# Order of blocks and expert rows on TensorE, fourteen more rows on VectorE, and a re-spaced block table, in a two-block model kernel

## The chip, the cores and the metric

The kernel runs on one NeuronCore of one Trainium2 chip. The metric is device time in microseconds (us) of one execution; lower is better. The kernel before takes 2434.16 us, the median of 3 runs (2432.61 to 2436.7).

## The reference: what is computed

512 tokens of width 1024 pass a first block (gated delta net, sparse attention and a gated feed-forward with a short causal convolution) and a second one (a pooling and a convolution branch, an output projection and an expert layer), all in float32. The parts that matter here are the first block's feed-forward, the second block's branches, and the expert layer, whose reference is, cut to its core:

```python
def chunk_fn(hc):                                   # 128 tokens, 8 heads, 16 experts per head
    q = (hc @ w_query).reshape(PEER_CHUNK, PEER_HEADS, PEER_KEY_DIM)
    s1 = jnp.einsum('chk,nk->chn', q[..., :PEER_HALF_DIM], keys_1)
    s2 = jnp.einsum('chk,nk->chn', q[..., PEER_HALF_DIM:], keys_2)
    ...                                             # two top-16 lists, their 256 sums, top 16 of these
    gate = jax.nn.softmax(top_s.astype(jnp.float32), axis=-1).astype(hc.dtype)
    u = jnp.take(expert_u, experts, axis=0)
    act = jax.nn.gelu(jnp.einsum('chkd,cd->chk', u, hc))
    v = jnp.take(expert_v, experts, axis=0)
    return jnp.einsum('chk,chkd->cd', gate * act, v)
```

Every token fetches 128 experts of its own, so 128 tokens by 2048 floats (u and v side by side, 1 MB) come in for each of 4 x 8 x 16 = 512 steps. Such a step is called a row below.

## The kernel before, in words

The 512 tokens are two halves of 256 (the weights are used once for each) and four chunks of 128. All causal work of the first half goes ahead, so the expert layer of chunks 0 and 1 can start while the second half still has to pass the first block's feed-forward and all of the second block. The program is written out by hand for each engine; there is no scheduler. A common clock ties the engines: the pair `p` of rows 2p and 2p+1, from 0 to 255, 64 pairs a chunk. For each pair

- GpSimd issues the indirect DMA of each row into one of `RING` = 9 buffers of 1 MB; row g waits until row g-9 has been used (L2772, in order);
- VectorE multiplies the u half with the token and sums (`row_dot`, L2600), one step of the search for the experts of the head after next (`route`), and then the second half's work of this pair (its `beside(p)`);
- ScalarE makes the two weights (gelu, times the gate, L1747 and L1751) and for a row that TensorE weighs a 128 x 128 diagonal matrix of them (L1755) (`weigh_pair`), and then its own `beside(p)`;
- TensorE adds the v half to two PSUM banks with the diagonal as the stationary operand (`row_pair`, two matmuls of 512 columns a row), and then does the second half's blocks of this pair (its `beside(p)`).

A row that is in the list `SIDE` is not weighed by TensorE but by VectorE, with one multiply-add of 128 x 1024 into a buffer `side` (`side_row`, L1873), in VectorE's `beside` two pairs later; one matmul pair with the identity adds `side` to PSUM at a chunk's end. `SIDE` is built of `ONE` (pairs whose second row is on VectorE) and `BOTH` (pairs whose first row is too). Before, it has 81 rows.

A block is 128 output columns of a weight matrix: 8 matmuls (6 for the last third of `down`) of 256 or 258 columns with weights of 512 KB from a ring of three slots, loaded by SyncE in the order of `weight_order()`. The tables say at which pair TensorE does which block: `UP_AT` and `DOWN_AT` (the feed-forward's 41 remaining up and 24 down blocks), `QUERY_AT`, `WIN_AT` (28 blocks of the second block's input projection), `BRANCH_AT`, `WOUT_AT`. What has to follow a block is placed some pairs behind it: ScalarE takes an up block out of PSUM at `at + 2`, VectorE finishes it at `at + 3` (`expanded`), a down block is added by VectorE at `at + 2` (`add_part`). TensorE may start block t only when the slot and the bank of block t-3 are free, that is when ScalarE or VectorE has taken block t-3 out (`weights`). A layer norm of the convolution branch stands at pairs 78 to 86: `ln_mean` (78) and `ln_var` (82) on TensorE, `ln_root` (84) on ScalarE, `ln_scale` (85) and `ln_silu` (86) on VectorE; it is followed by the branch blocks, whose pooling half for three blocks (`branch_pool`) is at pair 86.

Of the kernel before, what the change touches and what calls it, by code (L numbers as in the profile page):

```python
# [21 lines left out]
KT = D // P  # L22
# [59 lines left out]
EARLY = 8  # L82
EARLY_UP = 3
# [5 lines left out]

def ffn_at(i):  # L90

    return 1 + 7 * (i + min(KT, (i + 3) // 6)) // 12


UP_AT = [-1 if b < EARLY_UP else ffn_at(b if b < 24 else b + KT) for b in range(2 * FT)]
DOWN_AT = [ffn_at(24 + q if q < KT else 44 + q) for q in range(CHUNKS * KT)]
MID_AT = 47
# [4 lines left out]
BRANCH_AT = [87 + m // 2 for m in range(KT)]  # L102
WOUT_AT = [93 + m // 2 for m in range(KT)]
NORM_AT = 99
QUERY_AT = [{m: 1 + 7 * (7 * (m - EARLY) + 3) // 12 for m in range(EARLY, 16)},
            {m: (103, 104, 108, 110)[m] if m < 4 else 112 + 4 * (m - 4) for m in range(16)}]


ONE = [*range(1, 48), *range(52, 61), *range(83, 97)]
BOTH = [*range(4, 46, 4)]  # L110
SIDE = sorted([2 * p + 1 for p in ONE] + [2 * p for p in BOTH])


def sides(g):

    return sum(q < g for q in SIDE)
# [7 lines left out]
def tensor_rows(p):  # L124

    return [k for k in range(BATCH) if BATCH * p + k not in SIDE]


def weighed(p):

    return sum(bool(tensor_rows(q)) for q in range(p))
# [10 lines left out]
def weight_order():  # L142
# [5 lines left out]
    for p in range(NC * TILE):  # L148
        order += [("query", 0, m) for m, q in QUERY_AT[0].items() if q == p]
        order += [("up", 1, b) for b, q in enumerate(UP_AT) if q == p]  # L150
# [3 lines left out]
        order += [("w_out_2", 1, m) for m, q in enumerate(WOUT_AT) if q == p]  # L154
        order += [("query", 1, m) for m, q in QUERY_AT[1].items() if q == p]
    return order
# [36 lines left out]
def build(nc, a, out):  # L193
    ctx = ExitStack()
    with ctx:
# [402 lines left out]
        def _(pe):  # L598
            def mm(o, l, r, start=True, stop=True):
                return nc.tensor.matmul(o, l, r, start=start, stop=stop)  # L600
# [124 lines left out]
            for m in range(24):  # L725
                j = m % SLOTS
# [13 lines left out]
                if 11 <= m < 19:  # L740
                    i = m - 11
# [366 lines left out]
            def square_sum(s, k):  # L1108

                pe.wait_ge(sq3_ready, KT * s + k + 1)  # L1110
                if k == 0:
                    pe.wait_ge(ln_std, s // 2 + 1)
                    if s == 1:
                        pe.wait_ge(std3_ready, 1)
                mm(PS[:, 5, :HF], ones, sq4[:, k % 4, :], k == 0, k == KT - 1).then_inc(sq3_used, 1)
# [10 lines left out]
            def key_scores(s, m):  # L1126

                pe.wait_ge(q_ready, 16 * s + m + 1)
                if 16 * s + m:
                    pe.wait_ge(sc2_ready, 16 * s + m)  # L1130
                for c in range(2):
                    ins = mm(PS[:, 6, c * P:(c + 1) * P], qT[:, m % 2, c * P:(c + 1) * P],
                             mat("keys1") if m % 2 == 0 else mat("keys2"))
                ins.then_inc(sc2_done, 1)
# [8 lines left out]
            def row_pair(p, start, stop):  # L1143

                rows = tensor_rows(p)
                if rows and p < LAST:
                    pe.wait_ge(diag_ready, weighed(p + 1))
                if start:
                    pe.wait_ge(hr_ready, 4)
                    if p:  # L1150
                        pe.wait_ge(prow_ready, 2 * (p // TILE))
                for k in rows:
                    r = (p * BATCH + k) % RING
                    if p == LAST:
                        pe.wait_ge(diag_ready, weighed(p) + k + 1)
                    for v in range(2):
                        ins = mm(PS[:, v, :], diag[:, p % NB, k, :],
                                 ring_e[:, r, D + v * S:D + (v + 1) * S],
                                 start and k == 0, stop and k == BATCH - 1)
                        if v or (p == LAST and k):  # L1160
                            ins.then_inc(rows_used, 1)

            def side_sum(c):

                pe.wait_ge(side_used, sides(BATCH * TILE * (c + 1)))
                for v in range(2):
                    mm(PS[:, v, :], ident, side[:, v * S:(v + 1) * S], False, False)
# [64 lines left out]
            def beside(p):  # L1232
# [4 lines left out]
                for s in range(2):  # L1237
                    for m, at in QUERY_AT[s].items():
                        if p == at + 3:
                            key_scores(s, m)  # L1240
                for m, at in QUERY_AT[0].items():
                    if p == at:
# [27 lines left out]
                for m, at in enumerate(WOUT_AT):  # L1270
                    if p == at:
                        project_out(1, m)
                    if p == at + 3:
                        square_sum(2, m)
                for m, at in QUERY_AT[1].items():
                    if p == at:
# [13 lines left out]
            for p in range(NC * TILE):  # L1290
                if p in (TILE - 1, 2 * TILE - 1):
                    side_sum(p // TILE)
                row_pair(p, p % TILE == 0, p % TILE == TILE - 1)
                beside(p)


        @block.scalar
        def _(act):
# [485 lines left out]
            def beside(p):  # L1784
# [6 lines left out]
                for s in range(2):  # L1791
                    for m, at in QUERY_AT[s].items():
                        if p == at + 2:
# [1106 lines left out]
```

## Time and profile before

| what | before |
|---|---|
| median of 3 runs | 2434.16 us |
| the profiled execution, its own time | 2429.77 us |
| its span in the profile | 2428.1 us |
| TensorE busy (matmuls) | 2197.1 us, 90% |
| VectorE busy | 1663.0 us, 68% |
| ScalarE, GpSimd busy | 748.1 us, 632.2 us |
| HBM read | 750.59 MB |

The span is the time from the first to the last instruction that the profiler recorded; 1.7 us of the execution lie around it. Row work begins at 920.9 us (first indirect DMA issued) and fills the rest. TensorE is recorded with two MATMUL records for each float32 matmul of the program, so that a block is x16 and a row is x4 in the trace. Busy shares over the whole span mix stages with different limits; the views below are taken by stage. The time at which a matmul group starts after the one before it is its cost; the durations printed for a group also hold the pipeline's tail.

### The profile page before, as it was taken

Reading aid. Unit: us, or ns where it says so; the run is one execution under the profiler, and the core shown is the slowest. Engines: PE = TensorE matmul, PEld = TensorE weight load, DVE = VectorE, ACT = ScalarE, POOL = GpSimd, SP = SyncE. Lnnn points to the kernel's source line nnn. Section 1 sums busy time; section 2 is a strip of 40 time slices with the busy share of each in tenths; the row PEclk is TensorE's granted clock in tenths of the full one; section 3 lists DMA queues with packets and bytes.
Section 4 is the critical chain, followed back from the end, with each engine's and each line's share of the span. In section 5 each row is a group of like instructions: output and inputs, shape, how many; then the busy total and the mean of one; then the engine's idle time right before and its main releaser. Section 6 shows DMA issues by size and latency. Waiting matters only on the chain.

```text
span 2428.1 us, 25277 instructions
## 1 busy us (share of the span) xinstructions
PE 2197.1 (90%) x8236; PEld 1449.2 (60%) x8236; DVE 1663.0 (68%) x3734; ACT 748.1 (31%) x2109; POOL 632.2 (26%) x606
## 2 busy tenths in 40 slices
PE   7999998999999998999998999899888977778776
PEld 3444787788888886777774556565444432333332
DVE  5563645476657737988878998877666666676654
ACT  2321335421102212322324223244333333342322
POOL 1100000000110002323335343344434443444442
PEclk9999999999999999999999999999999999999999
DMA  8631020366774348999999999999999999999997
GB/s 344 200 120 56 32 70 1 111 230 223 266 271 148 132 156 349 414 401 380 398 400 420 413 395 379 370 404 420 421 420 421 422 421 421 419 417 420 421 415 306
DMA packets 131784, 754.22 MB, mean 311 GB/s; under 512 B 14544, under 2 KB 14672, under 8 KB 65616
## 3 DMA queue, kind: packets, MB, share of 16 engines
q0 software_dynamic: 87456, 588.90, 60.0%
q1 hardware_dynamic: 44208, 163.84, 18.6%
q8 instruction: 61, 1.00, 0.2%
q14 instruction: 59, 0.48, 0.1%
HBM read 750.59 MB, written 2.10 MB: 310 GB/s over the span
## 4 chain that ended last, share of the span: by engine, by line
PE 52%; DMA 27%; DVE 14%; ACT 4%; issue 2%; POOL 0%; DVEq 0%; SPq 0%; ACTq 0%; POOLq 0%
PE PS L600 51%; DMA arena<-experts_dram,ecur 23%; DVE arena L2600 4%; DVE arena L1873 3%; DVE h_all L1873 2%; DMA ring<-up_dram 1%; ACT const L1755 1%; DVE arena L1867 1%; ACT arena L1751 1%; ACT L1747 1%; DMA ring<-down_dram 1%; DMA ring<-branch_dram 1%; DVE h_all L1867 1%; DMA ring<-w_out_dram 1%; DMA xT<-x_dram 0%
## 5 line engine op out<-in xcount | busy, mean ns | idle before, releaser
L600 PE MATMUL PS<-arena,const 128*128 128x512 f32 (+2 forms) x1764 | 832.8, 618 | 170.4 <-ACT const L1755 161.5
L600 PE MATMUL PS<-h_all,ring 128*128 128x256 f32 (+2 forms) x3584 | 881.7, 403 | 13.9 <-DVE ring L1873 4.2
L2772 POOL DMA_INDIRECT arena<-experts_dram,ecur x512 | 583.0, 1139 | 1111.1 <-PE PS L600 702.4
L2600 DVE CUSTOM_DVE_ANT_0 arena<-arena 128x1024 f32<-128x1024 f32 x512 | 625.7, 1222 | 289.3 <-DMA arena<-experts_dram,ecur 286.0
L600 PEld LDWEIGHTS PS<-h_all,ring 128*128 128x128 f32 x3584 | 678.2, 190 | 224.9 <-issue 132.6
L600 PEld LDWEIGHTS PS<-arena,const 128*128 128x128 f32 x1764 | 335.4, 196 | 595.8 <-issue 345.7
L1747 ACT ACTIVATE arena<-arena 128x2 f32<-128x2 f32 x255 | 51.6, 202 | 727.6 <-DVE arena L2600 727.1
L600 PE MATMUL PS<-arena,ring 128*128 128x256 f32 x1088 | 243.7, 383 | 6.0 <-DMA ring<-down_dram 3.2
L600 PEld LDWEIGHTS PS<-arena,ring 128*128 128x128 f32 x1088 | 207.3, 192 | 39.6 <-DMA ring<-down_dram 5.1
L1755 ACT ACTIVATE const<-const,arena 128x128 f32<-128x128 f32 x429 | 148.4, 387 | 0.0
L600 PE MATMUL PS<-arena 128*128 128x128 f32 (+4 forms) x936 | 137.8, 299 | 8.5 <-DVE arena L1867 3.4
L600 PEld LDWEIGHTS PS<-arena 128*128 128x128 f32 (+2 forms) x936 | 118.0, 194 | 28.8 <-issue 12.8
L1924 DVE CUSTOM_DVE_ANT_0 arena<-arena 128x1024 f32<-128x1024 f32 x92 | 109.0, 1222 | 26.0 <-DMA arena<-ada_dram 24.7
L1751 ACT ACTIVATE arena<-arena 128x1 f32<-128x1 f32 x510 | 122.3, 287 | 8.4
L1873 DVE SCALAR_TENSOR_TENSOR arena<-arena 128x1024 f32<-128x1024 f32 (+3 forms) x118 | 107.8, 914 | 1.4
L1873 DVE SCALAR_TENSOR_TENSOR arena<-PS,param,arena 128x255 f32<-128x255 f32 (+3 forms) x128 | 72.3, 565 | 42.7 <-ACT arena L1376 31.7
L1873 DVE SCALAR_TENSOR_TENSOR xT<-PS,mod,xT 128x256 f32<-128x256 f32 x71 | 34.2, 482 | 96.4 <-PE PS L600 95.6
L2752 POOL DMA_DIRECT2D arena<-crow_dram x1 | 0.5, 528 | 316.1 <-ACT arena L1540 316.1
L2759 POOL DMA_DIRECT2D arena<-ada_dram x44 | 23.3, 529 | 222.2 <-DVE mod L1924 209.3
L1867 DVE TENSOR_TENSOR arena<-arena 128x512 f32<-128x512 f32 (+7 forms) x165 | 70.7, 429 | 5.2 <-ACT arena L1398 2.7
L1747 ACT ACT_TABLE_LOAD x37 | 47.5, 1283 | 65.1 <-DVE arena L2600 47.7
L1873 DVE SCALAR_TENSOR_TENSOR arena<-ring,param,arena 128x256 f32<-128x256 f32 x120 | 58.2, 485 | 4.3
(273 smaller groups left out, 1481.0 us busy)
## 6 DMA issues: line engine op xcount, KB each, us to landing
ring<-up_dram SPq DMA_DIRECT2D x88, 512.0 KB, 3.3
ring<-w_in_dram SPq DMA_DIRECT2D x80, 512.0 KB, 3.8
arena<-ada_dram POOLq DMA_DIRECT2D x80, 512.0 KB, 5.1
ring<-w_out_dram SPq DMA_DIRECT2D x32, 512.0 KB, 5.0
ring<-query_dram SPq DMA_DIRECT2D x32, 512.0 KB
ring<-down_dram SPq DMA_DIRECT2D x16, 704.0 KB, 5.8
ring<-branch_dram SPq DMA_DIRECT2D x16, 512.0 KB
arena<-experts_dram,ecur POOLq DMA_INDIRECT x512
```

The costliest lines, as they stand in the source:

```text
L600: return nc.tensor.matmul(o, l, r, start=start, stop=stop)
L1747: A(wts[:, b, :], dots[:, b, :], ACT.Gelu_apprx_tanh).then_inc(gelu_ready, 1)
L1751: A(wts[:, b, k:k + 1], wts[:, b, k:k + 1], ACT.Copy, scale=gcur[:, r % 3, j:j + 1]).then_inc(w_ready2, 1)
L1755: A(diag[:, b, k, :], ident, ACT.Copy, scale=wts[:, b, k:k + 1]).then_inc(diag_ready if k == rows[-1] else act_step, 1)
L1867: return V.tensor_tensor(out=o, in0=x, in1=y, op=op)
L1873: return V.scalar_tensor_tensor(out=o, in0=x, scalar=s_, in1=y, op0=op0, op1=op1)
L1924: V.tensor_tensor_reduce(out=w, in0=w, in1=row, scale=1.0, scalar=0.0, op0=MUL, op1=ADD, accum_out=mod[:, blk, t:t + 1]).then_inc(used, 1)
L2600: V.tensor_tensor_reduce(out=u, in0=u, in1=hrow[:, (r // HEADS) % 2, :], scale=1.0, scalar=0.0, op0=MUL, op1=ADD, accum_out=dots[:, p % NB ...
L2752: pool.dma_start(crow_2, a["crow"][1][:, 0:D]).then_inc(late_loaded, 16)
L2759: pool.dma_start(ring_2[:, j, :], a["ada_2"][bass.ds(i * SLOTS + j, 1)].rearrange("o p n -> p (o n)")).then_inc(slot_2_ready[j], 16)
L2772: nc.gpsimd.indirect_dma_start(out=ring_e[:, g % RING, :], out_offset=None, in_=a["experts"], in_offset=bass.IndirectOffsetOnAxis(ap=ecur[ ...
```

## The change

Three things change together. On TensorE, `beside(p)` is called before `row_pair(p)`, so the blocks of a pair stand ahead of the matmuls that weigh its rows. `SIDE` gets 14 more rows, nine in pairs 14 to 39 and five in pairs 81 to 99: 95 rows instead of 81. And the blocks of the feed-forward are spread at 5 blocks in 3 pairs from pair 1 on, where they stood at 12 blocks in 7 pairs from pair 3 on; the eight query blocks among them move by a pair at most.

```diff
 def ffn_at(i):
 
-    return 1 + 7 * (i + min(KT, (i + 3) // 6)) // 12
+    j = i - EARLY_UP
+    return 1 + 3 * (j + min(KT, (j + 3) // 6)) // 5
...
-QUERY_AT = [{m: 1 + 7 * (7 * (m - EARLY) + 3) // 12 for m in range(EARLY, 16)},
+QUERY_AT = [{m: 1 + 3 * (7 * (m - EARLY) + 3) // 5 for m in range(EARLY, 16)},
             {m: (103, 104, 108, 110)[m] if m < 4 else 112 + 4 * (m - 4) for m in range(16)}]
...
-ONE = [*range(1, 48), *range(52, 61), *range(83, 97)]
-BOTH = [*range(4, 46, 4)]
+ONE = [*range(1, 48), *range(52, 61), *range(81, 100)]
+BOTH = [*range(4, 46, 4), 14, 18, 19, 22, 23, 30, 34, 38, 39]
...
                 if p in (TILE - 1, 2 * TILE - 1):
                     side_sum(p // TILE)
+                beside(p)
                 row_pair(p, p % TILE == 0, p % TILE == TILE - 1)
-                beside(p)
```

The first place is TensorE at pairs 0 to 5, before. In these rows (instruction, what it writes and reads, columns, how many) `arena,const 128x512` is the weighing of rows, x2 for each, `h_all,ring 128x258` an up block (x8), `h_all,ring 128x256` a query block, and `mats,arena` the key scores:

```order
L600 MATMUL PS<-arena,const 128x512 x4
L600 MATMUL PS<-mats,arena 128x128 x2
L600 MATMUL PS<-arena,const 128x512 x4
L600 MATMUL PS<-h_all,ring 128x256 x8
L600 MATMUL PS<-arena,const 128x512 x2
L600 MATMUL PS<-h_all,ring 128x258 x24
L600 MATMUL PS<-arena,const 128x512 x2
```

And TensorE at pairs 0 to 5 in the changed kernel:

```order
L601 MATMUL PS<-mats,arena 128x128 x2
L601 MATMUL PS<-arena,const 128x512 x4
L601 MATMUL PS<-h_all,ring 128x258 x16
L601 MATMUL PS<-arena,const 128x512 x2
L601 MATMUL PS<-h_all,ring 128x256 x8
L601 MATMUL PS<-h_all,ring 128x258 x8
L601 MATMUL PS<-arena,const 128x512 x2
L601 MATMUL PS<-h_all,ring 128x258 x8
L601 MATMUL PS<-arena,const 128x512 x2
L601 MATMUL PS<-h_all,ring 128x258 x16
```

Two up blocks now stand between the rows of pair 0 and the row of pair 1, where before the rows of pairs 0, 1 and 2 stood together. Up to and with pair 4, six up blocks are done instead of three.

The second place is TensorE at pairs 81 to 87 before, where `sq,const 128x256` is `ln_var` and `h_all,ring 128x256` is an input projection block (x8) or the pooling half of three branch blocks (x12):

```order
L600 MATMUL PS<-arena,const 128x512 x4
L600 MATMUL PS<-h_all,ring 128x256 x8
L600 MATMUL PS<-arena,const 128x512 x4
L600 MATMUL PS<-h_all,ring 128x256 x8
L600 MATMUL PS<-sq,const 128x256 x4
L600 MATMUL PS<-arena,const 128x512 x8
L600 MATMUL PS<-h_all,ring 128x256 x12
L600 MATMUL PS<-arena,const 128x512 x2
```

And TensorE at pairs 81 to 87 in the changed kernel:

```order
L601 MATMUL PS<-h_all,ring 128x256 x8
L601 MATMUL PS<-arena,const 128x512 x2
L601 MATMUL PS<-h_all,ring 128x256 x8
L601 MATMUL PS<-sq,const 128x256 x4
L601 MATMUL PS<-arena,const 128x512 x8
L601 MATMUL PS<-h_all,ring 128x256 x12
L601 MATMUL PS<-arena,const 128x512 x2
```

Four matmuls, the rows of pair 82, went from before `ln_var` to behind it (one of them to VectorE), pair 81 keeps one row on TensorE, and the pooling halves now stand ahead of pair 86's row.

## Rows read from the trace of the kernel before

**Rows 1.** The page, busy time, share of the span and instructions of each engine.
```profile
PE 2197.1 (90%) x8236; PEld 1449.2 (60%) x8236; DVE 1663.0 (68%) x3734; ACT 748.1 (31%) x2109; POOL 632.2 (26%) x606
```

**Rows 2.** Windows of the row work: length, busy time by engine, TensorE's clock, DMA share, GB/s.
```profile
941.00:1300.00 359.00, 336.81 (x1364) 255.88 (x1364) 310.48 (x667) 110.12 (x321) 128.26 (x101) 0.99 1.00 401
1300.00:1500.00 200.00, 189.03 (x642) 122.45 (x643) 187.23 (x445) 63.13 (x205) 76.03 (x62) 0.98 1.00 400
1500.00:1550.00 50.00, 41.04 (x136) 27.06 (x135) 38.84 (x90) 16.22 (x46) 19.30 (x16) 0.90 0.95 367
1550.00:1700.00 150.00, 147.61 (x533) 95.88 (x532) 110.61 (x260) 56.72 (x166) 62.04 (x51) 1.00 1.00 408
1700.00:2350.00 650.00, 527.03 (x1272) 238.64 (x1272) 437.05 (x1088) 225.01 (x740) 266.48 (x253) 0.96 1.01 421
2350.00:2428.00 78.00, 55.61 (x122) 21.73 (x120) 37.97 (x64) 21.50 (x78) 22.42 (x23) 0.97 0.79 327
```

**Rows 3.** Windows, pairs 6 to 45, columns as in Rows 2.
```profile
960.00:1260.00 300.00, 290.86 (x1227) 229.30 (x1225) 258.08 (x543) 84.78 (x250) 102.11 (x82) 1.00 0.99 399
```

**Rows 4.** Timeline, TensorE, pairs 13 and 14: start, us, instruction, count.
```profile
1036.88 7.14 PE L600 MATMUL PS<-h_all,ring 128*128 128x258 f32 x32
1043.86 1.88 PE L600 MATMUL PS<-arena,const 128*128 128x512 f32 x4
1045.57 3.65 PE L600 MATMUL PS<-h_all,ring 128*128 128x258 f32 x16
```

**Rows 5.** Timeline, VectorE, pairs 14 to 18, columns as in Rows 4.
```profile
1025.59 1.23 DVE L2600 CUSTOM_DVE_ANT_0 arena<-arena 128x1024 f32<-128x1024 f32 x1
...
1045.88 2.04 DVE L1873 SCALAR_TENSOR_TENSOR ring<-PS,param,ring 128x256 f32<-128x256 f32 x4
...
1051.51 1.26 DVE L1873 SCALAR_TENSOR_TENSOR arena<-arena 128x1024 f32<-128x1024 f32 x1
...
1056.33 1.21 DVE L2600 CUSTOM_DVE_ANT_0 arena<-arena 128x1024 f32<-128x1024 f32 x1
```

**Rows 6.** Timeline, GpSimd, issue of row 37; in brackets idle time and releaser.
```profile
1046.01 0.94 POOL L2772 DMA_INDIRECT arena<-experts_dram,ecur  x1 [6.57 <-PE PS L600]
```

**Rows 7.** Waits, 950 to 1300 us: who for whom, us, times, longest.
```profile
POOL arena L2772 <- PE PS L600: 136.8, 31, 17.9
...
POOL arena L2772 <- DVE arena L1873: 88.9, 29, 8.0
...
DVE xT L1873 <- PE PS L600: 25.8, 10, 4.1
```

**Rows 8.** Timeline, VectorE, the second down block of pair 17.
```profile
1075.93 0.48 DVE L1873 SCALAR_TENSOR_TENSOR xT<-PS,mod,xT 128x256 f32<-128x256 f32 x1 [2.97 <-PE PS L600]
```

**Rows 9.** Timeline, TensorE, first rows of pair 0 and on.
```profile
946.10 5.08 PE L600 MATMUL PS<-arena,const 128*128 128x512 f32 x8 [7.17 <-ACT const L1755]
```

**Rows 10.** Timeline, GpSimd, issue of rows 11 and 13.
```profile
953.62 0.94 POOL L2772 DMA_INDIRECT arena<-experts_dram,ecur  x1 [1.01 <-PE PS L600]
...
956.26 0.95 POOL L2772 DMA_INDIRECT arena<-experts_dram,ecur  x1 [0.30 <-issue]
```

**Rows 11.** Timeline, TensorE, pairs 82 to 86.
```profile
1506.32 3.60 PE L600 MATMUL PS<-arena,const 128*128 128x512 f32 x8
1509.75 3.62 PE L600 MATMUL PS<-h_all,ring 128*128 128x256 f32 x16
1513.20 1.89 PE L600 MATMUL PS<-sq,const 128*128 128x256 f32 x8
...
1525.52 3.78 PE L600 MATMUL PS<-arena,const 128*128 128x512 f32 x4 [5.28 <-ACT const L1755]
```

**Rows 12.** Timeline, VectorE, pair 85's side row and the layer norm's scale.
```profile
1510.78 0.75 DVE L1870 TENSOR_SCALAR arena<-arena 128x1024 f32<-128x1024 f32 x1
1515.69 1.75 DVE L2406 RECIPROCAL rs<-rs 128x256 f32<-128x256 f32 x1 [4.17 <-ACT rs L1612]
```

## The prediction, made before the changed kernel had run

> **What bounds the kernel now.** I began with the page: TensorE is busy for 90% of the span and VectorE for 68% [rows 1]. That says little, since the change touches only pairs 0 to 99, so I went to windows of the row work and read the last column first. From 1700 to 2350 us nothing but rows is left and the DMA engines move 421 GB/s at a share of 1.01: full. That rate is my yardstick. A stretch of length T at a rate r holds T x (1 - r/421) of DMA time in which nothing was moved, and since the bytes are fixed this is the most that the stretch can give back [rows 2]:
>
> - 941 to 1300 us, the feed-forward of the second half: 359 x (1 - 401/421) = 17.1 us;
> - 1300 to 1500 us, input projection and convolution taps: 200 x (1 - 400/421) = 10.0 us;
> - 1500 to 1550 us, the layer norm: 50 x (1 - 367/421) = 6.4 us;
> - 1550 to 1700 us, branches and output projection: 150 x (1 - 408/421) = 4.6 us;
> - 1700 to 2350 us: none. What is won before 1700 us stays won, since full DMA work behind it only starts earlier.
>
> Who holds the DMA up? In pairs 6 to 45 (300 us) TensorE is busy for 290.9 us, VectorE for 258.1 us [rows 3]. TensorE's groups follow each other without a gap: two blocks from 1036.88 to 1043.86, so 3.49 us a block; one row from 1043.86 to 1045.57, so 1.71 us a row [rows 4]. GpSimd, which refills the ring, waited 136.8 us in 31 waits for TensorE to free a row buffer and 88.9 us in 29 for VectorE [rows 7]. So TensorE is the nearest bound here by a narrow margin: it is 97% busy, DMA runs at 95% of its yardstick.
>
> How far TensorE is behind shows in one pair. VectorE forms pair 14's first product at 1025.59; TensorE weighs that row at 1043.86, 18.3 us later, and ends at 1045.57; GpSimd then issues row 37 (nine rows on) at 1046.01, and VectorE reaches its product at 1056.33, 10.3 us after the issue [rows 4 to 6]. Meanwhile VectorE, at the end of pair 16, finishes the two up blocks of pair 13 at 1045.88, right after TensorE ended them at 1043.86 [rows 4, 5]. Its place is three pairs behind theirs, so TensorE's lag is as large as the tables allow. For a down block the place is only two pairs behind, and there VectorE must stop: 25.8 us in ten waits, one of them up to 1075.93 [rows 7, 8].
>
> From 1300 to 1500 us both TensorE (189.0 of 200 us) and VectorE (187.2) are nearly full [rows 2]; the change takes nothing from either there until pair 81.
>
> From 1500 us on it is the layer norm. TensorE weighs pair 82's two rows at 1506.32, does a block at 1509.75 and `ln_var` from 1513.20; ScalarE's root follows, and VectorE, which was done with its side row at 1510.78 + 0.75 = 1511.5, waits 4.17 us to 1515.69 [rows 11, 12]. TensorE then runs dry itself, 5.28 us before 1525.52, because pair 86's diagonal comes late [rows 11].
>
> **The change, part by part.**
>
> *Nine rows to VectorE in pairs 14 to 39.* TensorE: 9 x 1.71 = 15.4 us less. VectorE: 9 x 1.26 = 11.3 us more, by the side row at 1051.51 [rows 5]. VectorE has 300 - 258.1 = 41.9 us free in that stretch [rows 3], so the cover is there on the whole, but not at every pair. If the cover were gone the whole 11.3 us would lie on the path. Five of the nine are in pairs 14 to 23, around the first down blocks, and three in 34 to 39 around the next ones, where VectorE stood waiting for TensorE [rows 7, 8]. I take 2 us as given back, between 0 and 11.3.
>
> *Blocks before rows.* No work is added. Of what TensorE issues, only the order changes; the SyncE queue's weight loads keep their rule (free after block t-3) and change places only as the tables do. Two effects. (1) VectorE's and ScalarE's waits for a block end one row, 1.71 us, sooner against TensorE's rows. (2) A row buffer is freed behind its own pair's blocks, up to 2 x 3.49 = 7.0 us later. What queues behind that is GpSimd's in-order issue, and behind it the DMA engines. With TensorE at its allowed lag, row 2p+9 would be issued 7 us later against the product of pair p+4, and 10.3 us from issue to product [rows 5, 6] leaves no room. So VectorE's lead over TensorE must shrink from about three pairs to a little over two. That costs TensorE nothing as long as it still finds block t-3 taken out; I take 2 us for jitter in this narrower play, between 0 and 7 (one full lag of one pair).
>
> *Earlier start, even spacing.* Before, TensorE waits 7.17 us up to 946.10 for the first diagonal, then weighs the rows of pairs 0 to 2 together, and rows 11 and 13 are issued at 953.62 and 956.26 [rows 9, 10]. Now pair 1's row stands behind two blocks: row 11 about 7.0 us later. The blocks are work that has to be done anyway and TensorE was short of nothing else, but the row queue runs dry for part of it. The weights' loads fill some. I take 3 us, between 0 and 7.0.
>
> Sum for pairs 0 to 47: 15.4 - 2 - 2 - 3 = 8.4 us, under the cap of 17.1 us. From the bounds: 15.4 at best, 15.4 - 11.3 - 7 - 7 = -9.9 at worst.
>
> *Five rows to VectorE in pairs 81 to 99, and the new order at the layer norm.* `ln_var` comes after one row less of pair 81 (1.71 us) and before pair 82's rows, which took 1509.75 - 1506.32 = 3.43 us: 5.1 us sooner. VectorE's wait is 4.17 us and vanishes [rows 12]; its two more side rows there, 2 x 1.26 us, fall into pairs in which it waits for rows to land. So 4.2 us. The pooling halves of three branch blocks now fill TensorE's 5.28 us wait [rows 11], and pairs 97 to 99 lose 3 x 1.71 = 5.1 us on TensorE; at most 6.4 + 4.6 - 4.2 = 6.8 us more could come of it, but I see no wait that surely ends sooner, the branch blocks hanging on their weights. I take 0, between 0 and 6.8. If the cover fails on VectorE, 5 x 1.26 = 6.3 us come off.
>
> The sum is 8.4 + 4.2 = 12.6, say 12 us off the span of 2428.1 us: 2416 us, 2418 us for that execution. The median of the runs is 4.4 us above the profiled execution, so 2434.2 - 12 = 2422 us.
>
> **A page against the rows.** TensorE's 290.9 busy us of 300 are matmul time; its weight loads are 229.3 us, 76% [rows 3]. The Trainium skill (Trainium Kernel Development and Optimization, Performance Expectations) calls matmul busy time a poor measure of how near to its limit TensorE is, and the share of weight loads a good one. By that, TensorE had a quarter of its time free and the 15.4 us would buy nothing: the sum would be the 4.2 us of the layer norm alone. I side with the touching groups [rows 4], and keep it as a rival below. On DMA, the skill (DMA: Bandwidth & Descriptors, Specifications) gives one core about 358 GB/s from HBM; by it no stretch had anything to give back. The trace disagrees with 421 GB/s over 650 us [rows 2].
>
> **The rivals.**
>
> - *The gain stays in the ring.* The new order's later release costs both upper bounds (7 + 7 us) while the layer norm still pays: 15.4 - 14 - 2 + 4.2 = 3.6 us, 2431 us, no measurable change. For it: GpSimd already waits 136.8 us for TensorE. Against it: the lag shrinks instead of adding up. 15%.
> - *TensorE is not the limit* in pairs 6 to 45 and VectorE or DMA takes its place at once: 4.2 us, 2430 us. For it: three engines are within a few per cent of each other [rows 2, 3]. Against it: the long waits are for TensorE. 8%. (The skill's rule on weight loads, above, would come out here.)
> - *The ring becomes the loop, slower.* From a freed buffer: 0.4 us to the issue, 10.3 us to the product, some 4.5 us to the end of that pair on VectorE (1.2 for the product, 1.3 or 2.5 for side rows, 1 to 2 for the up blocks [rows 5]), two blocks 7.0 us, a row 1.7 us = 23.9 us, and that is a round of three pairs, where before, with rows ahead of blocks, it was one of four. 23.9 / 3 = 8.0 us a pair against 300 us / 40 = 7.5 us now. It decides when the issue takes more than about 9 us to become a product. Over the 28 pairs with up blocks: 28 x 0.5 = 14 us, less the layer norm's 4.2: 2444 us. Against it: with the DMA queue shorter a row lands sooner. 12%.
> - *Nearly all of the idle DMA time comes back*: 17.1 + 6.4 + 3 = 26 us, 2408 us. 5%.
>
> **Numbers.** The forecast, some 6 to 20 us off, has 60%; its own range is 2414 to 2428. Changes of 0.2%, 4.9 us, are about what a measurement of this kernel tells from none. Faster by more: 60 + 5 + 3 (parts of the first two) = 68%. Same: 12 + 8 = 20%. Slower: 12%. Leaving out the largest gain and most of the slow case gives 2412 to 2435.
>
> **What would show it.** Right: the rate from the first row to pair 47 rises from 401 to about 410 GB/s and pair 47 comes some 8 us sooner; TensorE's row records fall by 14 x 4; TensorE waits a little more and GpSimd's waits for it are more but shorter; VectorE's wait before its reciprocal of the layer norm is gone; the part behind 1700 us is the same at 421 GB/s, only shifted. Wrong: a first stretch at 401 GB/s or less, with VectorE waiting for rows to land (ring loop), or VectorE busy for over 96% (it took TensorE's place), or gaps of many us on TensorE that end with VectorE's take-out of an up block.

## The result, and the profile after: slower by 0.8%

The changed kernel takes **2452.1 us** (median of four runs, 2450.0 to 2453.4) where the kernel before takes 2433.4 us beside it (four runs, 2432.1 to 2436.7). The ratio is 1.0076, with a 95% interval of 1.0064 to 1.0089, or 15.6 to 21.7 us. The forecast was 2422 us with a range up to 2435; sign and size were both wrong. The profiled execution took 2453.36 us with a span of 2451.7 us.

The page's line of busy time, which answers to [rows 1]:

```profile
PE 2185.5 (89%) x8180; PEld 1444.9 (59%) x8180; DVE 1682.3 (69%) x3748; ACT 743.9 (30%) x2095; POOL 627.2 (26%) x606
```

TensorE lost 56 matmuls, the 14 x 4 of the fourteen rows, and 11.6 us of busy time. Yet the span grew by 23.6 us. The windows of the row work (columns as in [rows 2]) show where:

```profile
941.00:1300.00 359.00, 320.00 (x1296) 250.05 (x1296) 303.64 (x629) 93.28 (x280) 116.22 (x91) 0.96 0.96 375
1300.00:1500.00 200.00, 184.28 (x604) 116.18 (x604) 186.31 (x435) 66.68 (x205) 76.40 (x64) 0.97 1.00 404
1500.00:1550.00 50.00, 43.90 (x153) 28.63 (x152) 40.23 (x95) 19.48 (x55) 17.68 (x15) 0.99 0.95 368
1550.00:1700.00 150.00, 134.22 (x474) 90.55 (x474) 121.15 (x277) 49.96 (x150) 59.96 (x49) 0.93 0.99 397
1700.00:2350.00 650.00, 529.56 (x1326) 242.91 (x1325) 437.32 (x1100) 228.08 (x744) 268.69 (x255) 0.98 1.01 420
```

The first line answers for nearly all of it. From 941 to 1300 us DMA moved 375 GB/s where it had moved 401, so this stretch lacks 359 x (401 - 375) / 401 = 23.3 us of the old kernel's DMA work. The second moves a little more (404 against 400, 2.0 us), the third is as before, the fourth lacks 150 x (408 - 397) / 408 = 4.0 us, the fifth is as before. (From the second line on, the same window holds work that stands some 22 us later in the program.) TensorE, VectorE and DMA have all become *less* busy in the inner stretch that answers to [rows 3]:

```profile
960.00:1260.00 300.00, 272.96 (x1129) 217.46 (x1128) 251.14 (x513) 77.90 (x229) 94.66 (x76) 0.97 0.95 370
```

TensorE fell from 97% to 91%, VectorE from 86% to 84%, DMA from 399 to 370 GB/s. By the rate a pair now takes 7.5 x 399 / 370 = 8.1 us. All three are slower and none is full, which suggests that they wait for each other in a circle. The waits from 950 to 1300 us (who waits for whom, us in total, times, longest) answer to [rows 7]:

```profile
POOL arena L2773 <- PE PS L601: 192.6, 26, 18.2
...
POOL arena L2773 <- DVE arena L1874: 39.2, 15, 4.7
...
DVE arena L2601 <- DMA arena<-experts_dram,ecur: 29.5, 22, 5.0
...
PE PS L601 <- DVE ring L1874: 18.1, 8, 4.0
DVE xT L1874 <- PE PS L601: 15.3, 6, 6.0
```

Two of these waits were short in the kernel before:

```profile
DVE arena L2600 <- DMA arena<-experts_dram,ecur: 7.5, 7, 2.5
...
PE PS L600 <- DVE ring L1873: 4.2, 3, 1.6
```

VectorE waits 29.5 us for rows to land (7.5 before), TensorE 18.1 us for VectorE to take a block out (4.2 before). GpSimd waits 56 us more for TensorE to free a row and 50 us less for VectorE (88.9 before), so most of its idle time has only changed the engine that it is put down to. Follow one turn of the circle in the timelines (start, us, instruction, count, idle time and releaser). TensorE, pairs 11 to 15:

```profile
1038.94 1.88 PE L601 MATMUL PS<-arena,const 128*128 128x512 f32 x4
1040.66 10.63 PE L601 MATMUL PS<-h_all,ring 128*128 128x258 f32 x48
1051.12 1.88 PE L601 MATMUL PS<-arena,const 128*128 128x512 f32 x4
...
1061.47 8.79 PE L601 MATMUL PS<-h_all,ring 128*128 128x258 f32 x32 [4.00 <-DVE ring L1874]
1070.11 1.88 PE L601 MATMUL PS<-arena,const 128*128 128x512 f32 x4
```

GpSimd, the issues of rows 31 to 33 and of row 39 (row r goes into the buffer of row r - 9):

```profile
1041.10 1.05 POOL L2773 DMA_INDIRECT arena<-experts_dram,ecur  x1 [8.24 <-PE PS L601]
1042.45 1.09 POOL L2773 DMA_INDIRECT arena<-experts_dram,ecur  x1 [0.30 <-issue]
1043.84 0.94 POOL L2773 DMA_INDIRECT arena<-experts_dram,ecur  x1 [0.30 <-issue]
...
1072.26 0.94 POOL L2773 DMA_INDIRECT arena<-experts_dram,ecur  x1 [10.71 <-PE PS L601]
```

VectorE, the products of rows 31 to 33 and the take-out that ends pair 16:

```profile
1047.04 1.23 DVE L2601 CUSTOM_DVE_ANT_0 arena<-arena 128x1024 f32<-128x1024 f32 x1 [0.61 <-DMA arena<-experts_dram,ecur]
...
1051.52 1.23 DVE L2601 CUSTOM_DVE_ANT_0 arena<-arena 128x1024 f32<-128x1024 f32 x1 [0.85 <-DMA arena<-experts_dram,ecur]
...
1055.16 1.22 DVE L2601 CUSTOM_DVE_ANT_0 arena<-arena 128x1024 f32<-128x1024 f32 x1 [2.00 <-DMA arena<-experts_dram,ecur]
...
1060.32 2.04 DVE L1874 SCALAR_TENSOR_TENSOR ring<-PS,param,ring 128x256 f32<-128x256 f32 x4
```

TensorE weighs pair 11's row at 1038.94 and frees it at 1040.66. Row 31 goes out 0.4 us later, with rows 32 and 33 behind it; row 32's buffer had been free since VectorE's side row at 1032.12 + 1.28 = 1033.4, but GpSimd issues in order. VectorE waits for each of them to land (0.61, 0.85, 2.00 us), so pair 16's second product is at 1055.16 and, behind two side rows (one of them among the nine new ones), its take-out only at 1060.32. TensorE has stood 4.00 us for that take-out, does its blocks from 1061.47, and only behind them, at 1070.11, comes the row of pair 15. It is free at 1071.8, and row 39 goes out at 1072.26. From one freed row to the other are 31.2 us for four pairs: 7.8 us a pair, with nobody full. In the kernel before, the row stood ahead of the blocks, and TensorE's three waits for take-outs were 1.6 us at most.

TensorE's granted clock has a part in this. TensorE stands idle up to 1061.47, and then (columns as in [rows 2], the clock third from the end)

```profile
1061.40:1064.00 2.60, 2.52 (x6) 2.09 (x7) 2.50 (x7) 0.00 (x0) 0.15 (x1) 0.50 1.01 414
```

the clock is 0.50, that is 1.2 GHz instead of 2.4. The two blocks from 1061.47 to the row at 1070.11 cost 8.64 us where two blocks before cost 6.98 [rows 4]. Without these 1.66 us this turn would take 29.5 us, or 7.4 us a pair, about the pace of the kernel before: in this turn the circle's slack is used up, and the clock adds the loss. From 960 to 1260 us the clock fell so five times, each time when TensorE had just stood idle, for take-outs or for weights; in the kernel before it stayed at 1.00 there. As an estimate, the mean of 0.97 is worth at most 0.03 x 300 = 9 us of TensorE's time. So a part of the loss comes by way of the clock, as a consequence of the idle time; no run holds the two apart. A lower mean clock alone does not bring the loss: `f1_takeout`, below, has 0.96 from 941 to 1300 us as well (0.99 from 960 to 1260) and moves 398 GB/s against 375.

### The profile page after: what moved, and what is told of

Read it like the earlier page. It is cut to its first block, busy times and chain, and to the rows that moved or that the text cites. A ratio compares the mean times of both kernels' runs of the same rounds, so it can differ in the third digit from the quotient of the medians.

```text
span 2451.7 us, 25183 instructions
## 1 busy us (share of the span) xinstructions
PE 2185.5 (89%) x8180; PEld 1444.9 (59%) x8180; DVE 1682.3 (69%) x3748; ACT 743.9 (30%) x2095; POOL 627.2 (26%) x606
## 4 chain that ended last, share of the span: by engine, by line
PE 48%; DMA 28%; DVE 15%; ACT 4%; issue 3%; POOL 1%; DVEq 0%; SPq 0%; ACTq 0%; POOLq 0%
PE PS L601 48%; DMA arena<-experts_dram,ecur 25%; DVE arena L2601 4%; DVE arena L1874 4%; DVE h_all L1874 2%; DMA ring<-down_dram 2%; DVE arena L1868 1%; ACT const L1756 1%; ACT arena L1752 1%; DVE h_all L1868 1%; DMA ring<-up_dram 1%; POOL arena L2773 1%; ACT L1748 1%; DVE ring L1874 1%; DMA xT<-x_dram 0%
## 5 line engine op out<-in xcount | busy, mean ns | idle before, releaser
L601 PE MATMUL PS<-arena,const 128*128 128x512 f32 (+2 forms) x1708 | 804.9, 615 | 172.1 <-ACT const L1756 167.4
L601 PE MATMUL PS<-h_all,ring 128*128 128x256 f32 (+2 forms) x3584 | 891.9, 407 | 28.0 <-DVE ring L1874 23.9
L601 PEld LDWEIGHTS PS<-arena,const 128*128 128x128 f32 x1708 | 322.6, 196 | 586.6 <-issue 324.3
L601 PEld LDWEIGHTS PS<-arena,ring 128*128 128x128 f32 x1088 | 209.4, 194 | 47.1 <-DMA ring<-down_dram 12.7
L1874 DVE SCALAR_TENSOR_TENSOR arena<-arena 128x1024 f32<-128x1024 f32 (+3 forms) x132 | 125.7, 952 | 2.4
L2760 POOL DMA_DIRECT2D arena<-ada_dram x44 | 23.3, 529 | 222.1 <-DVE mod L1925 209.2
```

What stands on the lines that cost most here:

```text
L1874: return V.scalar_tensor_tensor(out=o, in0=x, scalar=s_, in1=y, op0=op0, op1=op1)
L2760: pool.dma_start(ring_2[:, j, :], a["ada_2"][bass.ds(i * SLOTS + j, 1)].rearrange("o p n -> p (o n)")).then_inc(slot_2_ready[j], 16)
```

## The experiments

"us" is (ratio - 1) x 2433.4. The last three columns come from the timelines: when VectorE starts its first product of the pair, counted from its first product of pair 0, minus the same in the kernel before. For pair 48 of the changed kernel these are the rows

```profile
940.47 1.23 DVE L2601 CUSTOM_DVE_ANT_0 arena<-arena 128x1024 f32<-128x1024 f32 x1
...
1301.08 1.22 DVE L2601 CUSTOM_DVE_ANT_0 arena<-arena 128x1024 f32<-128x1024 f32 x1
```

or 360.6 us, against 1279.07 - 940.61 = 338.5 us before: 22 us late.

| kernel | median, us | ratio (95%) | us | pair 8 | pair 48 | pair 255 |
|---|---|---|---|---|---|---|
| changed kernel | 2452.1 | 1.0076 (1.0064 to 1.0089) | +18.5 | +7.2 | +22.2 | +23.7 |
| e1_order | 2453.1 | 1.0088 (1.0067 to 1.0109) | +21.4 | +1.3 | +16.4 | +16.6 |
| e2_side | 2423.1 | 0.9952 (0.9936 to 0.9969) | -11.7 | -0.9 | -2.5 | -7.0 |
| e3_spacing | 2432.0 | 0.9986 (0.9976 to 0.9996) | -3.4 | +4.9 | +2.5 | +1.9 |
| e4_side_spacing | 2424.4 | 0.9960 (0.9946 to 0.9974) | -9.7 | +4.6 | -2.2 | -6.8 |
| f1_takeout | 2436.1 | 1.0011 (1.0000 to 1.0022) | +2.7 | +10.5 | +3.1 | +5.6 |
| f2_ring8_old | 2456.8 | 1.0086 (1.0069 to 1.0103) | +20.9 | +6.2 | +17.8 | +26.3 |
| f3_ring8_new | 2518.2 | 1.0331 (1.0305 to 1.0357) | +80.5 | +11.3 | +62.3 | +87.7 |
| f4_late | 2434.0 | 0.9999 (0.9987 to 1.0011) | -0.2 | +4.6 | +2.5 | +5.3 |
| f5_down | 2426.5 | 0.9970 (0.9961 to 0.9980) | -7.3 | +5.2 | 0.0 | -5.0 |
| f6_up | 2441.8 | 1.0046 (1.0030 to 1.0061) | +11.2 | +6.9 | +13.4 | +8.5 |
| f7_norm | 2423.2 | 0.9962 (0.9951 to 0.9973) | -9.2 | +4.6 | -2.4 | -10.2 |
| g1_side_early | 2420.7 | 0.9948 (0.9930 to 0.9969) | -12.7 | +3.6 | -2.5 | -8.8 |

The profile columns come from one execution each. Up to pair 47 `e4_side_spacing` and `f4_late` are the same program and differ by 4.7 us at pair 48: differences below about 5 us between two kernels in those columns say little. Inside one profile, from one pair to another, a step that returns in several kernels says more.

### The parts apart: e1_order, e2_side, e3_spacing, e4_side_spacing

`e1_order` is the kernel before with

```diff
+                beside(p)
                 row_pair(p, p % TILE == 0, p % TILE == TILE - 1)
-                beside(p)
```

> Only the new order on TensorE (blocks of a pair ahead of its rows), tables and side rows as before. Theory A (the ring loop: a row buffer is freed one pair's blocks later, so 9 buffers are too few) expects most or more of the whole loss: 15 to 35 us slower than before, since TensorE has no relief from side rows. Theory B (the fourteen side rows overload VectorE) expects no change within 5 us. Theory C (the earlier start of the blocks starves the row queue) expects at most 5 us slower.

`e2_side` is the kernel before with the fourteen rows alone:

```diff
-ONE = [*range(1, 48), *range(52, 61), *range(83, 97)]
-BOTH = [*range(4, 46, 4)]
+ONE = [*range(1, 48), *range(52, 61), *range(81, 100)]
+BOTH = [*range(4, 46, 4), 14, 18, 19, 22, 23, 30, 34, 38, 39]
```

> Only the fourteen more side rows, order and tables as before. Theory A expects 4 to 12 us faster than before, by TensorE's 15.4 us of relief in the first stretch. Theory B expects 10 to 20 us slower. Theory C expects no loss, 0 to 10 us faster.

`e3_spacing` is the kernel before with the spacing alone:

```diff
-    return 1 + 7 * (i + min(KT, (i + 3) // 6)) // 12
+    j = i - EARLY_UP
+    return 1 + 3 * (j + min(KT, (j + 3) // 6)) // 5
...
-QUERY_AT = [{m: 1 + 7 * (7 * (m - EARLY) + 3) // 12 for m in range(EARLY, 16)},
+QUERY_AT = [{m: 1 + 3 * (7 * (m - EARLY) + 3) // 5 for m in range(EARLY, 16)},
```

> Only the new spacing of the feed-forward's blocks (from pair 1, five in three pairs), order and side rows as before. Theory A expects within 5 us of before. Theory B expects the same. Theory C expects 8 us slower or more.

`e4_side_spacing` has both of these and the old order; it is the changed kernel with `beside(p)` put back behind `row_pair`.

> The changed kernel without its new order on TensorE: side rows and spacing. Theory A expects faster than before by 4 to 12 us, so some 25 us faster than the changed kernel. Theory B and theory C expect it slower than before, near the changed kernel's 2452 us.

Measured: the order alone costs 21 us, the side rows gain 12, the spacing gains 3. Side rows and spacing together gain 10, and the order put on top of them costs 28. The sum of the three parts would be +6.3; all together are +18.5, so the order is dearer with the other two than without. The windows from 960 to 1260 us, first of `e1_order`, then of `e2_side`:

```profile
960.00:1260.00 300.00, 282.98 (x1178) 222.96 (x1176) 247.58 (x518) 81.48 (x239) 91.95 (x77) 0.98 0.96 377
```
```profile
960.00:1260.00 300.00, 286.25 (x1212) 228.14 (x1211) 272.73 (x556) 82.45 (x244) 111.30 (x83) 0.99 1.00 402
```

The order alone does to this stretch most of what the whole change did: 377 GB/s and TensorE at 94%, with TensorE waiting 15.8 us for take-outs and VectorE 38.2 us for rows to land (950 to 1300 us). So the order is the culprit, and neither the side rows nor the start are: by pair 8 `e1_order` is 1.3 us late.

`e2_side` tells a second thing. TensorE has less to do and is at 95%, VectorE at 91%, and DMA moves 402 GB/s instead of 399, at a share of 1.00. By pair 48 only 2.5 us are won, of the nine rows' 15.4. The rest is won where the layer norm is; VectorE's reciprocal, which waited 4.17 us [rows 12], waits 0.71:

```profile
1513.24 1.75 DVE L2406 RECIPROCAL rs<-rs 128x256 f32<-128x256 f32 x1 [0.71 <-ACT rs L1612]
```

From pair 80 to 88 `e2_side` goes from 4.0 to 7.5 us ahead; `e4_side_spacing`, `f5_down` and `f7_norm` gain 3.5, 3.5 and 3.7 us in the same eight pairs.

### Does the circle run through the take-outs and the ring? f1_takeout, f2_ring8_old, f3_ring8_new

If the circle is the cause, shortening it at another place must give time back, and taking a buffer out of it must cost more in the new order than in the old one. `f1_takeout` is the changed kernel with the second half's feed-forward take-outs one pair sooner on VectorE and ScalarE:

```diff
-                    if p == at + 2 and m >= EARLY_UP:
+                    if p == at + 1 and m >= EARLY_UP:
...
-                    if p == max(UP_AT[2 * t], UP_AT[2 * t + 1]) + 4:
+                    if p == max(UP_AT[2 * t], UP_AT[2 * t + 1]) + 3:
...
-                    if p == at + 3 and m >= EARLY_UP:
+                    if p == at + 2 and m >= EARLY_UP:
```

The `tanh_gate`, `square_block(1, ...)` and `add_part` lines lose one pair in the same way.

> The changed kernel with ScalarE's and VectorE's work on the feed-forward's up and down blocks one pair earlier (taken out at the block's pair + 1, finished at + 2, down blocks added at + 1). If the loss is a round of ring and take-outs (free buffer, issue, landing, product, take-out, block, rows), this gives the round one pair more, and TensorE's idle time falls: 10 to 25 us faster than the changed kernel's 2452 us. If the late release by itself costs the time, whoever waits behind it, the take-outs' place changes nothing beyond 5 us. If VectorE then has to wait for TensorE at each block instead, it is slower than the changed kernel by 5 us or more.

`f2_ring8_old` is `e4_side_spacing`, `f3_ring8_new` the changed kernel, each with

```diff
-RING = 9
+RING = 8
```

> Side rows and spacing with the old order, and a ring of 8 row buffers instead of 9 (against 2424 us with 9). The ring theory expects a cost already here, 3 to 12 us, as half a pair of the play is gone. A theory in which the ring is deep enough in either order expects under 3 us.

> The changed kernel (new order) with a ring of 8 row buffers instead of 9 (against 2452 us with 9). The ring theory expects that the lost buffer costs clearly more than under the old order: 15 to 40 us more than the changed kernel. If the loss is TensorE standing at its blocks' waits and not the ring, it costs about what it costs under the old order.

Measured: `f1_takeout` gives 16 us of the 28 back. Its window and its waits, 950 to 1300 us:

```profile
960.00:1260.00 300.00, 287.41 (x1223) 228.88 (x1222) 269.44 (x551) 82.34 (x247) 112.73 (x83) 0.99 0.99 397
```
```profile
POOL arena L2773 <- DVE arena L1874: 116.0, 33, 7.3
...
POOL arena L2773 <- PE PS L601: 99.8, 21, 18.6
...
DVE arena L2601 <- DMA arena<-experts_dram,ecur: 7.3, 9, 1.7
...
PE PS L601 <- DVE ring L1874: 5.1, 2, 2.9
```

TensorE's wait for take-outs fell from 18.1 to 5.1 us, VectorE's for rows from 29.5 to 7.3, and GpSimd's for TensorE from 192.6 to 99.8. No work was removed and TensorE's order of blocks and rows is the same; only VectorE's and ScalarE's work on the blocks stands a pair earlier, and all three waits shrank together. This is what a circle through the take-outs predicts. The control, the same edit in the old order, was not run; in `e4_side_spacing` TensorE waited 3.2 us for take-outs in one wait, so there was little for it to shorten. By pair 48 `f1_takeout` is 3.1 us behind the kernel before instead of 22.2. Of the 12 us that it stays over `e4_side_spacing`, its profile has 5 us at pair 48, all of them there since the first eight pairs, and 7 us behind pair 48, where the edit does not reach.

One buffer fewer costs 30.6 us in the old order and 62 us in the new. The direction is the expected one, both sizes are missed: the theory had 3 to 12 and 15 to 40 us. So nine buffers were a tight ring in the old order too. The windows of `f2_ring8_old` and `f3_ring8_new`, and of `f3_ring8_new` the waits:

```profile
960.00:1260.00 300.00, 279.33 (x1170) 222.32 (x1169) 259.66 (x529) 78.96 (x230) 97.56 (x76) 0.98 0.98 383
```
```profile
960.00:1260.00 300.00, 253.42 (x1019) 200.36 (x1017) 227.81 (x464) 71.16 (x209) 81.83 (x68) 0.93 0.88 335
```
```profile
DVE arena L2601 <- DMA arena<-experts_dram,ecur: 62.6, 37, 4.6
...
PE PS L601 <- DVE ring L1874: 45.3, 12, 6.3
```

With eight buffers both waits of the circle more than double (29.5 to 62.6, 18.1 to 45.3 us), and DMA is down to 335 GB/s. The old order with eight buffers (383 GB/s) still beats, from 960 to 1260 us, the new order with nine (370): there the new order costs more than a buffer of the ring.

### In which pairs? f4_late, f5_down, f6_up, f7_norm

These are `e4_side_spacing` with the new order in some pairs only:

```diff
+                if COND:
+                    beside(p)
                 row_pair(p, p % TILE == 0, p % TILE == TILE - 1)
-                beside(p)
+                if not (COND):
+                    beside(p)
```

COND is `p >= 48` in `f4_late`, pairs 16 to 20 and 35 to 44 (down blocks) in `f5_down`, pairs 1 to 15 and 21 to 34 (up blocks) in `f6_up`, and pairs 82 and 86 (the layer norm's) in `f7_norm`.

> Side rows and spacing, with the new order on TensorE only from pair 48 on. The ring theory places the whole loss in pairs 0 to 47, so it expects the time of side rows and spacing alone, 2424 us, within 4 us. If the new order also pays at the layer norm, as the prediction had it, 2 to 5 us faster than 2424. If the order costs in the branches too (blocks two a pair there), 3 to 8 us slower.

> Side rows and spacing, with the new order on TensorE only in the pairs of down blocks (16 to 20, 35 to 44). A down block is taken out a pair earlier than an up block, so the round through ring and take-outs is a pair longer there. The ring theory expects a small share of the first stretch's 24 us: 0 to 8 us slower than side rows and spacing alone (2424 us). If the order costs the same wherever it stands, 8 to 10 us.

> Side rows and spacing, with the new order on TensorE only in the pairs of up blocks (1 to 15, 21 to 34). The ring theory expects most of the first stretch's 24 us here: 14 to 24 us slower than 2424 us. If the order costs the same wherever it stands, 15 us; if the down pairs are the dear ones (TensorE then is nearest to VectorE), under 10 us.

> Side rows and spacing, with the new order on TensorE only in pairs 82 and 86: ln_var ahead of pair 82's row, the pooling halves ahead of pair 86's. The prediction's step on the layer norm expects up to 4 us below side rows and spacing alone (2424 us), if the side rows have not already taken that wait. The ring theory, by which the late part of the new order costs through the rows of pairs 79 to 83 that are freed later, expects no loss here: within 3 us of 2424.

Measured against `e4_side_spacing` (-9.7 us): `f6_up` +20.9, `f4_late` +9.5, `f5_down` +2.4, `f7_norm` +0.5. The first three cover nearly all pairs, and their sum, 32.8, is near the 28 us of the new order everywhere. Windows of `f6_up`, then of `f5_down`:

```profile
960.00:1260.00 300.00, 276.58 (x1155) 219.72 (x1154) 257.98 (x527) 78.35 (x229) 96.03 (x78) 0.98 0.97 381
```
```profile
960.00:1260.00 300.00, 284.44 (x1210) 226.23 (x1209) 269.84 (x550) 82.50 (x245) 113.11 (x81) 0.99 1.00 400
```

So the up pairs carry it. `f5_down` cannot be told from `e4_side_spacing` (their intervals overlap), though it puts blocks ahead of rows in 15 pairs. `f7_norm` shows no gain and no cost from the order at the layer norm itself that could be told from none. `f4_late` missed its expectation: the theory had placed the whole loss in pairs 0 to 47 and allowed 4 us. The late part is only half settled: the ten runs of `f4_late` lie between 2426 and 2439 us, and in its profile 4.7 of 12.1 us against `e4_side_spacing` stand there before the programs differ. It goes from 2.5 us late at pair 48 to 5.3 at the end while `e4_side_spacing` goes from 2.2 to 6.8 ahead, so 7.4 us lie behind pair 48, not in pairs 82 and 86 themselves. Its profile has most of them at one place: `f4_late` is 2.7 us late at pair 83 and 8.9 at pair 84, while `e4_side_spacing` goes from 2.7 to 1.8 us ahead and `f7_norm` from 3.6 to 2.7; `f1_takeout` and the changed kernel make the same step of 6.4 us. Before it GpSimd in `f4_late` had waited for TensorE to free pair 78's row,

```profile
1490.01 1.05 POOL L2776 DMA_INDIRECT arena<-experts_dram,ecur  x1 [7.85 <-PE PS L601]
```

which points at the same late release in the input projection's pairs 78 to 80. No run tried the order in these pairs alone.

### Who limits once the old order is back? g1_side_early

`e4_side_spacing` with VectorE's side rows a pair sooner, so that it frees them sooner:

```diff
-                for g in range(BATCH * (p - 2), BATCH * (p - 1)):
+                for g in range(BATCH * (p - 1), BATCH * p):
```

> Side rows and spacing with the old order, and VectorE's side rows one pair earlier (pair p - 1 instead of p - 2), so that the buffers of these 95 rows are free a pair sooner. The ring theory expects a gain, 2 to 8 us below 2424 us, since GpSimd waited 112 us for VectorE's rows there; if VectorE instead has to wait for ScalarE's weights, 5 us slower or more.

GpSimd's waits, 950 to 1300 us, of `e4_side_spacing` and then of `g1_side_early`:

```profile
POOL arena L2773 <- DVE arena L1874: 112.1, 31, 10.6
...
POOL arena L2773 <- PE PS L601: 106.8, 24, 18.3
```
```profile
POOL arena L2773 <- PE PS L601: 181.7, 33, 18.5
...
POOL arena L2773 <- DVE arena L1874: 30.6, 12, 5.8
```

81.5 us of waiting for VectorE went away and 74.9 us of waiting for TensorE came in their place: the same idle time under another name. The time is 2420.7 us, the lowest here, 0.5% below the kernel before (interval 0.3 to 0.7%); against `e4_side_spacing` the intervals overlap, and the gain is not told from none. In this kernel DMA moved 405 GB/s from 941 to 1300 us, the most of all fourteen kernels.

## Why the prediction was wrong, step by step

**The step that failed: "blocks before rows".** It said: "That costs TensorE nothing as long as it still finds block t-3 taken out; I take 2 us". TensorE did not find it taken out. The order cost 21 us alone and 28 us with the rest, where I allowed 0 to 7. The error was to treat the later release as a shift that is paid once, "one full lag of one pair". A release that is late in every pair is paid in every pair as soon as the way from it back to itself has no slack. All parts of that way stood in the prediction: the in-order issue, the landing, the product, the take-out, the block that waits for it. The rival on the ring followed them round; the sum followed them up to the product and stopped. What the runs showed instead is TensorE waiting 18.1 us for take-outs where it had waited 4.2, and a loss in every turn.

**The rival "the ring becomes the loop" was what happened.** It gave 8.0 us a pair; the rate says 8.1. It priced the loop at 14 us over 28 pairs with up blocks; from pair 8 to 48 the changed kernel lost 22.2 - 7.2 = 15 us. That both come out so near is in part luck, since the turn is another one than it drew. It had a round of three pairs and 23.9 us. The turn in the timelines spans four pairs: 0.4 us to the issue, 14.1 to row 33's product (row 33 waits in the queue behind rows 31 and 32), 6.3 to the block that gets its bank back, 8.6 for two blocks, 1.7 for the row, 31.2 us in all with the 1.66 us of slow clock, on which the rival had nothing. It even named the pairs, which `f6_up` and `f5_down` bear out. It had 12%, because "with the DMA queue shorter a row lands sooner". That came true in part: row 31 needed 5.9 us from issue to product, rows 32 and 33, queued behind it, 9.1 and 11.3. It did not open the circle, since the take-out of the whole pair waits for the last of them. What the rival lacked beside this were the start (7.2 us at pair 8) and a price behind pair 48; it took off 4.2 us there.

**Nine side rows: mis-sized.** I took 15.4 - 2 = 13.4 us. By pair 48 `e2_side` is 2.5 us ahead, in one profile. Here the yardstick was wrong. I read 401 GB/s against 421 as idle DMA time of 17.1 us, though the share of DMA in that same row was 1.00. In none of fourteen kernels did that stretch pass 405 GB/s. The mean hides two kinds of time. The rate of the kernel before in 40 slices of 9 us, 941 to 1300 us:

```profile
GB/s 418 374 417 422 419 418 415 420 419 395 391 419 423 412 378 367 409 258 428 414 410 394 405 362 424 414 362 411 416 383 369 422 421 401 316 425 416 417 424 424
```

25 of the 40 slices stand at 410 or more, with weights coming in beside the rows, and eight below 380. That weights are in the traffic does not by itself set the lower mean. The kernel before moved 400 GB/s from 1300 to 1500 us, with 13.1 of 79.9 MB on the weights' queue (16%); `f7_norm` moved 419 from 1550 to 1700 us, with 9.3 of 62.8 MB (15%):

```profile
1550.00:1700.00 150.00, 141.95 (x502) 90.38 (x501) 112.61 (x259) 57.27 (x167) 64.38 (x54) 0.98 1.01 419
```

What makes the low slices stays open. So the second rival, that something else takes TensorE's place at once, describes the side rows in the feed-forward. The Trainium skill (Trainium Kernel Development and Optimization, Performance Expectations), by which matmul busy time is a poor measure of TensorE's nearness to its limit, would have come out nearer than my reading of the touching groups did. What it gives as the better measure, the share of weight loads, this case does not test: it stood at 76% before and what stood beside it once TensorE had less to do was a DMA share of 1.00.

**Layer norm: 4.2 us, right in size, wrong in cause.** `e2_side` gains 3.5 us from pair 80 to 88, and the 4.17 us wait shrinks to 0.71 with the old order. That pair 81 and its neighbours have a row less on TensorE is the likely reason; the new order added nothing (`f7_norm`). In the changed kernel the wait is gone too, but VectorE then waits for rows to land. Its rows there:

```profile
1535.94 1.23 DVE L2601 CUSTOM_DVE_ANT_0 arena<-arena 128x1024 f32<-128x1024 f32 x1 [1.68 <-DMA arena<-experts_dram,ecur]
...
1538.44 1.75 DVE L2407 RECIPROCAL rs<-rs 128x256 f32<-128x256 f32 x1
```

**Earlier start, even spacing: 3 us lost, 0 to 7.** By medians the spacing alone gains 3.4 us. In its profile it is 4.9 us late at pair 8 and 1.9 at the end, which does not agree in sign. One profile has a play of some 5 us, so the medians decide, and their interval stays only just below 1: small, and on the side of a gain. With the order the start costs 7.2 us by pair 8. Row 11 is issued 8.1 us later than in [rows 10], and 13 is later by 14.1:

```profile
961.67 1.79 POOL L2773 DMA_INDIRECT arena<-experts_dram,ecur  x1 [7.32 <-PE PS L601]
...
970.33 1.16 POOL L2773 DMA_INDIRECT arena<-experts_dram,ecur  x1 [5.63 <-PE PS L601]
```

**Right:** the matmul count, VectorE's vanished wait, 420 GB/s behind 1700 us, and the first sign named for wrong: a first stretch at 401 GB/s or less with VectorE waiting for rows to land. GpSimd's waits for TensorE, which were to be more and shorter, became fewer and longer: 26 waits with a mean of 7.4 us against 31 of 4.4.

**The sum, as measured** (ratios, us): side rows -11.7, spacing -3.4, order alone +21.4, and +12.2 that only appear together. The intervals of the parts are 2 to 5 us wide on each side, so this last figure is sure in its sign and rough in its size. With the order the side rows no longer help. In the turn above the take-out stands behind two side rows on VectorE, one of them new, so a new side row also lengthens the circle by its 1.26 us; that the three act through the same circle is the likely reason and was not taken apart further.

## What to carry to other kernels

Where an engine frees a ring buffer and also waits for what that ring feeds, as TensorE does here, add up the whole circle (free, issue, landing, use, take-out, back to the freeing instruction) and divide by the steps that it spans: if that is above the present pace (here 8.0 us against 7.5), a later release is paid in every step and not once. Let the sum follow the queue: in the turn measured, the row that counted was the third of three issued together, and the turn spanned a pair more. The test is cheap: take one buffer out in either order, or move a take-out one step; here the price of the buffer doubled with the change. Read the DMA share of a window beside its rate: from 941 to 1300 us a share of 1.00 went with 401 GB/s, and no kernel here got more than 405 out of it. It is no proof of a limit: from 1550 to 1700 us the kernel before moved 408 at 1.00 and `f7_norm` 419 at 1.01.

## What the runs showed that I had not expected

- With nine buffers and the old order up to pair 47, DMA moved 397 to 405 GB/s at a share of 0.99 to 1.00 from 941 to 1300 us, and 420 to 421 at 1.01 from 1700 to 2350 us, where nearly all traffic is rows. When the circle starves it, share and rate fall unequally: 375 GB/s at 0.96, 335 at 0.88. The share does not tell how many bytes are missing.
- Waiting can change its name without changing its amount: in `g1_side_early` 81.5 us of GpSimd's waits left VectorE and 74.9 us came to TensorE.
- A wait of 4.00 us for a take-out cost TensorE another 1.66 us, since its granted clock was 0.50 for the first 3 us of the blocks behind it.
- One of nine row buffers is worth 30.6 us in the old order and 62 us in the new.
